# Ten conditioning slots multiplied inside the two layers, and expert slots of 4 MB in a ring of three

## The chip, the cores and the metric

The kernel is one program on one core of a Trainium2 chip. The metric is the device time of one execution in microseconds. Three executions of the kernel before took 2242.32, 2244.37 and 2247.17 us.

## The reference

A token matrix `x` (256 x 1024, fp32) goes through two layers of a first block and then through one layer of a second block.

```
layer l of the first block (l = 0, 1):
    h = rmsnorm(x);  s = h @ w_in            # 1024 -> 3072, cut in 12 slices of 256 columns
    cat = [depthwise conv, stick-breaking attention, retention, short conv](s)
    x = x + rmsnorm(cat @ w_out)             # 1024 -> 1024
    x = x + rmsnorm(ffn(rmsnorm(x)))         # ffn_up, conv over time, gating, ffn_down
second block:
    mod  = silu(c)     @ ada_w + ada_b       # 1024 -> 6144: shift 1, scale 1, gate 1, shift 2, scale 2, gate 2
    modc = silu(c_ctx) @ ada_w + ada_b
    u = modulate(rmsnorm(x), sh1, sc1);  uc = modulate(rmsnorm(ctx), sh1c, sc1c)
    y = token_mixer(u, uc);  x = x + g1 * y
    x = x + g2 * moe(modulate(rmsnorm(x), sh2, sc2))   # 32 experts, 4 of them for each token
    return rmsnorm(x)
```

`mod` and `modc` depend on `c`, `c_ctx` and the weights alone, on nothing that the first block computes. `ada_w` is 24 MB in fp32; the kernel cuts it into twelve slots of 512 columns (2 MB each), called 0 to 11 here.

## The kernel before

**Weights and their ring.** SyncE loads all weights in one fixed order. In the layers and in the mixer of the second block the unit of loading is a half slot of 1 MB; five places form a ring (`RING`), and half `g` waits in `half_used` until half `g - 5` has been used. `LAYER_SLOTS` and `B2_SLOTS` give the order. For the weights of `in`, `up` and `down`, used means split: ScalarE rounds a unit (a quarter of a slot) into a high part (L901, in the second block L995), VectorE subtracts to get the low part (L1231, L1401), and TensorE multiplies in three passes (`PASSES`). Three units are buffered, so `split_until(n)` runs up to three units ahead of TensorE. For `out` used means that the output projection has read it: the first slot at `slot_free`, the second when the bank `("M", 3)` is filled. For an `ada` slot it means that its product is done. Every engine works through its own list in order, so a wait on SyncE or ScalarE holds up all that stands behind it.

**A layer.** `project(0)` to `project(5)` make the twelve slices (items `("s", i)`), with small attention matmuls between. Then come `("I", h)`, `("SB", c)`, the output projection in four parts into banks 4 to 7 (items `("M", i)`, `tokens_down`), with `("CM", 0)` and `("CV", 0)` for the norm of the conv branch between them. After it ScalarE and VectorE both execute

```
split_until(MIX_UNITS + UNIT_BUFFERS - 1)      # units 24, 25, 26: those of ("up", 0)
rms_of_banks(l, "M")                           # ScalarE L868; on VectorE: add_normed, then normalise
```

while TensorE runs filler matmuls (`keep_clock`), waits for the new `x` and for its normalised rows, transposes them (`("F", i)`, L1832), runs filler again, and starts the FFN (66 units with eleven rounds of gating).

**The second block.** TensorE multiplies slots 0 to 3 first, stacked in four column groups of 32 (`ada`). ScalarE copies each result out, `ada_follow` turns it into columns of `modT` with four narrow matmuls (shift and scale), or adds its four partial rows and spreads the sum over all partitions with one wide matmul (gate, slots 4, 5, 10, 11). VectorE adds the bias (L1421) and makes `scale1` and `shift1` (L1434, L1435), which the splits, the modulated rows `u_rows` and so the first projection `mq` wait for. Slots 4 to 11 are multiplied between the projections `mq`, `mk`, `mv` and `mo`.

**The experts.** Sixteen pairs of experts pass through one loop. The whole ring region (12 MB) then holds six places of 2 MB; piece `(w1, x, q)` or `(w2, x, q)` is a quarter or a half of the matrix of expert `x` of the pair. TensorE computes both experts side by side in the two halves of the array and waits for both pieces of a step `q` together (`expert_slot`, L726). SyncE waits on `expert_slot_free` for each place (L807 to L810).

## Time and profile before

| | |
|---|---|
| three executions | 2242.32, 2244.37, 2247.17 us |
| the profiled execution, its own time | 2252.0 us |
| its span, first to last instruction | 2250.2 us |
| TensorE busy | 2079.9 us (92%) |
| VectorE, ScalarE busy | 847.5 us, 651.96 us |
| moved from HBM | 587.27 MB |
| two layers | about 0 to 693 us |
| second block up to the experts | about 699 to 1297 us |
| expert loop | about 1297 to 2239 us |

The page of the profile gives busy times over the whole span; a window gives them for a stretch, with the granted clock of TensorE (1.00 is full speed) and what the DMA moved. A timeline row merges like instructions that follow one another: start, length, engine, line, operation, tile written and tiles read, count, and in brackets the idle time just before with what ended it. The chain of waits lists, in order of time, which work each piece of the span was spent on, followed back from the last instruction. TensorE's helpers record nearly all matmuls at one line (L1812), so the tiles tell them apart: `small` as an input is `siluc`, the operand of the conditioning products.

### The profile page before, as it was taken

Reading aid. Unit: us, or ns where it says so; the run is one execution under the profiler, and the core shown is the slowest. Engines: PE = TensorE matmul, PEld = TensorE weight load, DVE = VectorE, ACT = ScalarE, POOL = GpSimd, SP = SyncE. Lnnn points to the kernel's source line nnn. Section 1 sums busy time; section 2 is a strip of 40 time slices with the busy share of each in tenths; the row PEclk is TensorE's granted clock in tenths of the full one; section 3 lists DMA queues with packets and bytes.
Section 4 is the critical chain, followed back from the end, with each engine's and each line's share of the span. In section 5 each row is a group of like instructions: output and inputs, shape, how many; then the busy total and the mean of one; then the engine's idle time right before and its main releaser. Section 6 shows DMA issues by size and latency. Waiting matters only on the chain.

```text
span 2250.2 us, 28318 instructions
## 1 busy us (share of the span) xinstructions
PE 2079.9 (92%) x11092; PEld 1342.4 (60%) x11092; DVE 847.5 (38%) x1477; ACT 652.0 (29%) x1008; POOL 11.6 (1%) x23
## 2 busy tenths in 40 slices
PE   8899999889998998899999999999999999999997
PEld 7859997849995776776789533333333333333332
DVE  5757676566765334653622211111111111111112
ACT  4435555435555323242431201111111111111111
POOL 0000000000000000000000000000000000000000
PEclk9999999999998999999999999999999999999998
DMA  7325544426546444011233579999999999999995
GB/s 282 113 107 194 187 165 148 142 107 202 183 167 254 173 182 178 29 73 41 93 113 150 243 334 424 417 413 424 422 426 425 429 428 421 430 428 429 421 430 252
DMA packets 55822, 589.63 MB, mean 262 GB/s; under 512 B 6640, under 2 KB 7328, under 8 KB 10000
## 3 DMA queue, kind: packets, MB, share of 16 engines
q1 hardware_dynamic: 53984, 583.09, 63.9%
q0 software_dynamic: 1456, 5.01, 0.8%
q8 instruction: 63, 1.03, 0.2%
q10 hardware_dynamic: 288, 0.24, 0.0%
q14 instruction: 31, 0.25, 0.0%
HBM read 587.27 MB, written 1.05 MB: 261 GB/s over the span
## 4 chain that ended last, share of the span: by engine, by line
PE 73%; DMA 15%; DVE 6%; issue 3%; ACT 2%; SPq 0%; DVEq 0%; ACTq 0%
PE psum L1812 45%; PE psum L2209 20%; DMA slots<-exp_w_dram 14%; PE psum L2199 3%; PE psum L2224 2%; PE psum L2309 2%; DVE split_weights L1401 1%; ACT work L868 0%; DVE work L1527 0%; DMA slots<-ffn_up_dram 0%; DVE split_weights L1231 0%; DVE split_rows L1209 0%; PE psum L2120 0%; SPq L810 0%; PE psum L1832 0%
## 5 line engine op out<-in xcount | busy, mean ns | idle before, releaser
L2209 PE MATMUL psum<-slots,work 128*64 128x512 f32 x3072 | 688.4, 603 | 69.8 <-DMA slots<-exp_w_dram 69.8
L2209 PEld LDWEIGHTS psum<-slots,work 128*64 128x64 f32 x3072 | 227.8, 138 | 506.7 <-issue 506.7
L1812 PE MATMUL psum<-split_rows,split_weights 128*128 128x256 f32 (+1 forms) x3744 | 494.2, 294 | 23.0 <-DVE split_weights L1231 10.2
L1812 PEld LDWEIGHTS psum<-split_rows,split_weights 128*128 128x128 f32 x3744 | 476.9, 194 | 44.5 <-issue 12.8
L1231 DVE TENSOR_TENSOR split_weights<-slots,split_weights 128x1024 fp32r<-128x1024 f32 x180 | 219.0, 1223 | 154.9 <-ACT split_weights L901 154.1
L901 ACT ACTIVATE split_weights<-slots 128x1024 fp32r<-128x1024 f32 x180 | 189.8, 1058 | 224.8 <-PE psum L1812 187.3
L1812 PE MATMUL psum<-split_weights,split_rows 128*128 128x512 f32 x1008 | 234.7, 393 | 2.3 <-DVE split_weights L1401 2.3
L882 ACT ACTIVATE work<-psum 128x512 f32<-128x512 f32 (+2 forms) x180 | 94.6, 537 | 434.6 <-PE psum L2209 291.3
L1812 PEld LDWEIGHTS psum<-split_weights,split_rows 128*128 128x128 f32 x1008 | 190.0, 190 | 44.4 <-DVE split_weights L1401 2.7
L1812 PE MATMUL psum<-work 128*128 128x128 f32 (+9 forms) x992 | 159.3, 341 | 23.0 <-DVE work L1563 6.9
L1771 DVE TENSOR_SCALAR work<-psum 128x512 f32<-128x512 f32 x32 | 22.0, 688 | 406.1 <-PE psum L2209 406.1
L1812 PEld LDWEIGHTS psum<-work 128*128 128x128 f32 (+2 forms) x992 | 130.0, 201 | 55.6 <-issue 40.3
L1146 ACT ACTIVATE work<-work 128x512 f32<-128x512 f32 x32 | 20.2, 631 | 475.4 <-DVE work L1771 475.4
L1766 DVE TENSOR_SCALAR work<-psum,small 128x128 f32<-128x128 f32 x64 | 21.9, 404 | 281.8 <-PE psum L1812 281.8
L1401 DVE TENSOR_TENSOR split_weights<-slots,split_weights 128x1024 fp32r<-128x1024 f32 x64 | 76.4, 1221 | 110.4 <-ACT split_weights L995 110.3
L995 ACT ACTIVATE split_weights<-slots 128x1024 fp32r<-128x1024 f32 x64 | 66.8, 1055 | 111.2 <-DMA slots<-w_in_dram 63.8
L1812 PE MATMUL psum<-slots,work 128*128 128x512 f32 x192 | 87.3, 614 | 3.2 <-ACT work L882 1.6
L1812 PE MATMUL psum<-const 128*128 128x384 f32 (+2 forms) x218 | 76.5, 495 | 11.2 <-DVEq L1804 6.7
L1370 DVE SCALAR_TENSOR_TENSOR work<-psum,work 128x254 f32<-128x254 f32 (+1 forms) x176 | 76.6, 477 | 1.6
L1812 PEld LDWEIGHTS psum<-slots,work 128*128 128x128 f32 x192 | 37.4, 197 | 49.2 <-issue 47.1
L2199 PE MATMUL psum<-work 128*128 128x512 f32 (+1 forms) x136 | 65.8, 627 | 0.5 <-ACT work L882 0.5
L1812 PEld LDWEIGHTS psum<-const 128*128 128x128 f32 (+1 forms) x218 | 41.3, 198 | 41.2 <-issue 15.8
(237 smaller groups left out, 1330.0 us busy)
## 6 DMA issues: line engine op xcount, KB each, us to landing
slots<-exp_w_dram SPq DMA_DIRECT2D x192, 2048.0 KB, 16.3
slots<-w_in_dram SPq DMA_DIRECT2D x56, 1024.0 KB, 5.0
slots<-ffn_up_dram SPq DMA_DIRECT2D x44, 1024.0 KB, 4.8
slots<-ada_w_dram SPq DMA_DIRECT2D x24, 1024.0 KB, 7.0
slots<-ffn_down_dram SPq DMA_DIRECT2D x20, 1024.0 KB, 4.8
slots<-w_out_dram SPq DMA_DIRECT2D x12, 1024.0 KB, 4.9
slots<-w_branch_a_dram SPq DMA_DIRECT2D x4, 1024.0 KB, 8.0
slots<-w_branch_b_dram SPq DMA_DIRECT2D x4, 1024.0 KB, 5.1
```

Of the source, the lines that this page charges most:

```text
L882: nc.scalar.activation(out_, in_, func, **kw).then_inc(evacuated[bank_of(key)], 1)
L901: nc.scalar.activation(unit_weights(n, 0), raw, ACT.Copy).then_inc(w_high_ready, 1)
L995: nc.scalar.activation(unit_weights2(n, 0), unit_weights2(n, None), ACT.Copy).then_inc(w_high_ready, 1)
L1231: nc.vector.tensor_tensor(unit_weights(n, 1), unit_weights(n, None)[0], unit_weights(n, 0), ALU.subtract).then_inc(w_split, 1)
L1370: ins = nc.vector.scalar_tensor_tensor(out=o, in0=b[:, c * T:(c + 1) * T - k], scalar=cols[:, at:at + 1], in1=o, op0=ALU.mult, op1=ALU.add)
L1401: nc.vector.tensor_tensor(unit_weights2(n, 1), unit_weights2(n, None), unit_weights2(n, 0), ALU.subtract).then_inc(w_split, 1)
L1771: nc.vector.tensor_scalar(glu[n], take(dve, ("GLU", n), it), LIMIT, None, ALU.min).then_inc(evacuated[bank_of(("GLU", n))], 1)
L1812: return nc.tensor.matmul(out_, lhsT, rhs, start=first, stop=last)
L2199: return nc.tensor.matmul(psum[:, i, :], lhsT, rhs, start=first, stop=True, skip_group_check=True)
L2209: return nc.tensor.matmul(b[rows, :], lhs[:, rows], rhs, start=first, stop=last, skip_group_check=True)
L2224: nc.tensor.matmul(b, pick_e, b1_rows[:, c0:c0 + 512], start=True, stop=False, skip_group_check=True)
L2309: ins = nc.tensor.matmul(b[:, c * T:(c + 1) * T], hT_split[:, v, 4 * j + k, c * P:(c + 1) * P], wu[a][:, k, :], start=j + c + k + q == 0, ...
```

## The change

`ada_w` is reordered on the host so that ten slots come first; five are multiplied in each of the two layers (`modulation`), from slots `mod` that are put into `LAYER_SLOTS`. The products of mod 0 and mod 1 stand inside `project(4)` and `project(5)`, those of mod 2 and 3 behind the output projection, in place of six filler matmuls, and that of mod 4 with the columns of the second pair behind the FFN's transposes, in place of five. ScalarE copies the results out (`mod_rows_out`), `modulation_columns` turns four of them into columns of `modT`, and the fifth of each layer is one half of gate 1, kept in `g1_kept`. Silu of `c` moves into the layer. Slots 10 and 11 (gate 2) stay where they were in the second block; slots 0 to 9 leave it. In the expert loop the matrices of a pair are interleaved on the host, so that one load of 4 MB brings the pieces of both experts for a step; six loads a pair go through three places in place of twelve through six.

```diff
-LAYER_SLOTS = [("in", s) for s in range(6)] + [("out", s) for s in range(2)]
+N_MOD = 5
+LAYER_SLOTS = [("in", s) for s in range(5)] + [("mod", 0), ("in", 5), ("mod", 1), ("out", 0), ("out", 1)]
+LAYER_SLOTS += [("mod", i) for i in (2, 3, 4)]
+OUT_SLOT = LAYER_SLOTS.index(("out", 0))
+FFN_SLOT = len(LAYER_SLOTS)
...
-LAYER_BANKS += [("s", 6, 6), ("s", 7, 7), ("RQ", 0, 0), ("RK", 0, 1), ("s", 8, 2), ("s", 9, 3)]
+LAYER_BANKS += [("s", 6, 6), ("s", 7, 7), ("RQ", 0, 0), ("RK", 0, 1), ("s", 8, 2), ("mod", 0, 4), ("s", 9, 3)]
 LAYER_BANKS += [("RS", h, 4 + h) for h in range(4)]
-LAYER_BANKS += [("s", 10, 0), ("s", 11, 1)]
+LAYER_BANKS += [("s", 10, 0), ("mod", 1, 2), ("s", 11, 1)]
 LAYER_BANKS += [("I", h, 2 + h) for h in range(4)]
 LAYER_BANKS += [("RO", 0, 0), ("SB", 0, 6), ("SB", 1, 7)] + [("M", i, 4 + i) for i in range(4)]
-LAYER_BANKS += [("CM", 0, 1), ("CV", 0, 2), ("RT", 0, 3)]
-LAYER_BANKS += [("F", i, i) for i in range(4)]
+LAYER_BANKS += [("CM", 0, 1), ("MT", 0, 3), ("CV", 0, 2), ("RT", 0, 3)]
+LAYER_BANKS += [("mod", 2, 0), ("mod", 3, 1)] + [("F", i, i) for i in range(4)] + [("mod", 4, 4), ("MT", 1, 5), ("MT", 2, 6)]
 LAYER_BANKS += [("U", g, (2 * (g // 2)) % 4 + g % 2) for g in range(6)]
...
-B2_BANKS += [("ada", 0, 0), ("ada", 1, 1), ("mT", 0, 2), ("ada", 2, 0), ("ada", 3, 1)]
 B2_BANKS += [("XT", i, i) for i in range(4)] + [("CT", i, 4 + i) for i in range(4)]
-B2_BANKS += [("mq", 0, 0), ("mq", 1, 1), ("ada", 4, 6), ("ada", 5, 7)] + [("mk", h, 2 + h) for h in range(4)]
-B2_BANKS += [("mg", 0, 6), ("mR", 4, 0), ("mR", 5, 1), ("gates", 0, 2), ("ada", 6, 2), ("ada", 7, 3)]
+B2_BANKS += [("mq", 0, 0), ("mq", 1, 1)] + [("mk", h, 2 + h) for h in range(4)]
+B2_BANKS += [("mg", 0, 6), ("gates", 0, 2)]
 B2_BANKS += [("mv", i, 4 + i) for i in range(4)]
-B2_BANKS += [("F", 9, 0), ("GT", 0, 1), ("GT", 1, 2), ("mT", 1, 3), ("ada", 8, 0), ("ada", 9, 1)]
+B2_BANKS += [("F", 9, 0), ("GT", 0, 1), ("GT", 1, 2)]
 B2_BANKS += [("mv", 4 + i, 4 + i) for i in range(4)]
 B2_BANKS += [("ada", 10, 2), ("ada", 11, 0)] + [("mo", i, 4 + i) for i in range(4)]
...
 
-PAIR_SLOTS = [("w1", x, q) for q in range(4) for x in (0, 1)] + [("w2", x, q) for q in range(2) for x in (0, 1)]
+PAIR_SLOTS = [("w1", q) for q in range(4)] + [("w2", q) for q in range(2)]
 PLACE_OF_HALF = {s: i for i, s in enumerate((5, 6, 7, 8, 9, 10, 11, 3, 4, 0, 1, 2))}
-PAIR_RING = 6
+PAIR_RING = 3
 PACKED_KINDS = [slot for slot in B2_SLOTS if slot[0] not in ("ada", "wa", "wb", "wo")]
 
...
-            elif l == L2 or LAYER_SLOTS[n][0] == "out":
+            elif l == L2 or LAYER_SLOTS[n][0] in ("out", "mod"):
...
 
-            at = WEIGHTS_AT + 2 * HALF * (n % PAIR_RING)
-            return slots[:, at:at + 2 * HALF]
+            at = WEIGHTS_AT + 4 * HALF * (n % PAIR_RING)
+            return slots[:, at:at + 4 * HALF]
 
         def expert_slot(pe, it, n, n_k):
 
             pe.wait_ge(expert_loaded[n % PAIR_RING], 16 * (2 * it) + 16 * (n // PAIR_RING + 1))
-            rows = expert_place(n).rearrange("p (k n) -> p k n", k=n_k)
-            return lambda k, c0, c1: rows[:, k, c0:c1]
+            rows = expert_place(n).rearrange("p (x k n) -> p x k n", x=2, k=n_k)
+            return [lambda k, c0, c1, xx=xx: rows[:, xx, k, c0:c1] for xx in (0, 1)]
...
+                elif kind == "mod":
+                    two = [w["ada_w_2"][N_MOD * l + s, h] for h in (0, 1)]
...
             def pair(it, j):
-                for n, (kind, xx, q) in enumerate(PAIR_SLOTS):
-                    src = w["exp_w1_2" if kind == "w1" else "exp_w2_2"][2 * j + xx, q]
-                    sp.wait_ge(expert_slot_free, 12 * it + (n + 1))
+                for n, (kind, q) in enumerate(PAIR_SLOTS):
+                    src = w["exp_w1_2" if kind == "w1" else "exp_w2_2"][j, q]
+                    sp.wait_ge(expert_slot_free, 6 * it + (n + 1))
...
                 evac(("s", 7), l, flat(rv), take(act, ("s", 7), l))
+                act.wait_ge(c_loaded, 16)
+                act.wait_ge(zeros_ready, 3)
+                nc.scalar.activation(siluc[:, :, 0:2], cT, ACT.Silu).then_inc(siluc_ready, 1)
 
                 act.wait_ge(sb_abs, l + 1)
...
+                mod_rows_out(0)
                 evac(("s", 9), l, flat(sc_b), take(act, ("s", 9), l))
...
+                mod_rows_out(1)
                 act.wait_ge(sb_arg, l + 1)
...
                 evac(("RT", 0), l, flat(catT[:, 4:6, :]), take(act, ("RT", 0), l))
                 split_until(MIX_UNITS + UNIT_BUFFERS - 1)
                 rms_of_banks(l, "M")
+                mod_rows_out(2)
+                mod_rows_out(3)
                 rms_of_x(l, 2 * l + 2)
                 act.wait_ge(ffn_par_loaded, 32 * l + 32)
                 high_rows("F", l, 4, COL_FFN_PRE)
+                take(act, ("MT", 1), l)
+                mod_rows_out(4)
 
...
-                act.wait_ge(c_loaded, 16)
-                act.wait_ge(zeros_ready, 3)
-                nc.scalar.activation(siluc[:, :, 0:2], cT, ACT.Silu).then_inc(siluc_ready, 1)
                 def split(n):
                     if n >= UNIT_BUFFERS:
...
-                ada_follow(0)
-                ada(2)
-                ada_follow(1)
-                ada(3)
-                ada_follow(2)
-
-                ada_follow(3)
...
-                        wt = [expert_slot(pe, it, 2 * q + xx, 2) for xx in (0, 1)]
+                        wt = expert_slot(pe, it, q, 2)
...
-                                elif (k, i) == (1, 3):
+                                elif xx and (k, i) == (1, 3):
                                     ins.then_inc(expert_slot_free, 1)
...
                     return ins
 
-                def project(s):
+                def modulation(i):
+
+                    wt = slot_ready(pe, LAYER_SLOTS.index(("mod", i)), l, KC)
+                    if i == 0:
+                        pe.wait_ge(siluc_ready, l + 1)
+                    b = fill(pe, ("mod", i), l)
+                    for k in range(KC):
+                        q = k % 4
+                        ins = mm(b[32 * q:32 * q + 32, :], siluc[:, k, :], wt(k, 0, 512), k < 4, k >= 4)
+                    done(ins, ("mod", i))
+
+                def modulation_columns(i):
+
+                    for j in (2 * i, 2 * i + 1):
+                        after_evacuation(pe, ("mod", j), l)
+                    b = fill(pe, ("MT", i), l)
+                    for c in range(8):
+                        ins = mm(b[:, 2 * c:2 * c + 2], mod_buffers[2 * i + c // 4][:, (c % 4) * P:(c % 4 + 1) * P], mod_pick)
+                    done(ins, ("MT", i))
+
+                def project(s, between=None):
 
                     for i in (2 * s, 2 * s + 1):
+                        if i % 2 and between is not None:
+                            modulation(between)
                         b = fill(pe, ("s", i), l)
                         for j in (0, 1):
                             n = 2 * i + j
...
                 for c in (0, 1):
                     diagonal_scores("RS", l, rkT, rqT, c)
...
                 pe.wait_ge(sb_soft, l + 1)
...
                 mm(b[:, 0:T], ones, conf_sq[:, 0, :], True, False)
                 done(mm(b[:, 0:T], ones, conf_sq[:, 1, :], False, True), ("CV", 0))
                 pe.wait_ge(sc_cat, l + 1)
-                tokens_down("M", l, 7, catT, (6, 7), False, False, None)
+                tokens_down("M", l, OUT_SLOT + 1, catT, (6, 7), False, False, None)
...
-                keep_clock(("F", 0), l, 6)
+                tokens_down("M", l, OUT_SLOT + 1, catT, (4, 5), False, True, None)
+
+                modulation(2)
+                modulation(3)
                 pe.wait_ge(x_tile_ready, 2 * l + 2)
-                keep_clock(("F", 0), l, 3)
-                transposed("F", l, 2, idle=(("D", 0), 5))
+                keep_clock(("F", 2), l, 3)
+                transposed("F", l, 2, idle=lambda: (modulation(4), modulation_columns(1)))
                 for n in range(MIX_UNITS, len(UNITS)):
                     slot, j = UNITS[n]
+                    if n == MIX_UNITS + 1:
+                        after_evacuation(pe, ("mod", 4), l)
+                        b = fill(pe, ("MT", 2), l)
+                        done(mm(b, mod_spread, mod_buffers[4]), ("MT", 2))
                     kind, g = LAYER_SLOTS[slot]
```

## Rows read from the trace of the kernel before

**Rows 1.** The page: TensorE's busy time, and the chain that ended last, by engine.

```profile
PE 2079.9 (92%) x11092; PEld 1342.4 (60%) x11092; DVE 847.5 (38%) x1477; ACT 652.0 (29%) x1008; POOL 11.6 (1%) x23
...
PE 73%; DMA 15%; DVE 6%; issue 3%; ACT 2%; SPq 0%; DVEq 0%; ACTq 0%
```

**Rows 2.** Windows: stretch, length, busy time of each engine, clock, DMA share, GB/s.

```profile
1960.00:2016.00 56.00, 51.42 (x240) 20.70 (x238) 8.58 (x17) 7.51 (x12) 0.00 (x0) 1.00 1.01 429
```

**Rows 3.** The chain of waits in layer 0: start, length, what.

```profile
138.25 4.79 DMA slots<-ffn_up_dram
...
144.09 1.10 ACT work L868 x2
```

**Rows 4.** Timeline of SyncE's DMA issues in the same stretch.

```profile
138.25 8.14 SPq L780 DMA_DIRECT2D slots<-ffn_up_dram  x5
```

**Rows 5.** Timeline of TensorE in the same stretch.

```profile
122.55 1.13 PE L1812 MATMUL psum<-work,const 128*128 128x256 f32 x4 [1.58 <-ACT work L941]
...
131.18 13.90 PE L1812 MATMUL psum<-slots,work 128*128 128x512 f32 x32
...
155.76 3.39 PE L1812 MATMUL psum<-const 128*128 128x384 f32 x10
```

**Rows 6.** Windows with queued loads: 1 MB (two windows), then 2 MB.

```profile
148.00:152.00 4.00, 3.16 (x9) 1.26 (x8) 3.90 (x6) 1.35 (x3) 0.00 (x0) 1.00 1.00 418
...
820.00:832.00 12.00, 12.00 (x55) 9.90 (x54) 5.26 (x10) 2.47 (x3) 0.00 (x0) 1.00 1.01 427
1240.00:1264.00 24.00, 24.00 (x58) 10.61 (x57) 3.30 (x4) 2.52 (x4) 0.00 (x0) 1.00 1.02 434
```

**Rows 7.** Timeline of TensorE in layer 1, slices 9 and following.

```profile
423.51 3.14 PE L1812 MATMUL psum<-split_rows,split_weights 128*128 128x256 f32 x24 [1.87 <-DVE split_weights L1231]
...
435.26 13.28 PE L1812 MATMUL psum<-split_rows,split_weights 128*128 128x256 f32 x96 [2.51 <-DVE split_weights L1231]
```

**Rows 8.** Timeline of ScalarE: the Silu of `c`.

```profile
697.72 1.28 ACT L990 ACT_TABLE_LOAD   x1
699.02 0.23 ACT L990 ACTIVATE small<-small 128x16 f32<-128x16 f32 x1
```

**Rows 9.** Timeline of VectorE at the start of the second block.

```profile
707.60 0.76 DVE L1430 TENSOR_SCALAR work<-work,stats 128x1024 f32<-128x1024 f32 x1
720.80 0.19 DVE L1421 TENSOR_TENSOR small<-psum,work 128x32 f32<-128x32 f32 x1 [12.44 <-PE psum L1812]
...
721.25 0.16 DVE L1435 SCALAR_TENSOR_TENSOR small<-small,work 128x8 f32<-128x8 f32 x1
```

**Rows 10.** Windows in the second block, for the granted clock.

```profile
704.00:708.00 4.00, 0.04 (x1) 0.07 (x1) 2.10 (x5) 3.22 (x8) 0.00 (x0) 0.67 1.00 422
812.00:816.00 4.00, 4.00 (x23) 2.67 (x26) 1.91 (x5) 0.00 (x0) 0.00 (x0) 0.50 0.00 0
```

**Rows 11.** Timeline of TensorE: products, spreads and columns between the projections.

```profile
746.01 3.64 PE L1812 MATMUL psum<-slots,small 128*32 128x512 f32 x32
...
775.17 2.79 PE L1812 MATMUL psum<-work 128*128 128x512 f32 x12
778.37 3.64 PE L1812 MATMUL psum<-slots,small 128*32 128x512 f32 x32 [0.41 <-DVE small L1463]
...
810.80 3.41 PE L1812 MATMUL psum<-work 128*128 128x2 f32 x16
814.14 5.53 PE L1812 MATMUL psum<-slots,small 128*32 128x512 f32 x32
...
841.50 1.84 PE L1812 MATMUL psum<-work 128*128 128x2 f32 x16
```

**Rows 12.** Timeline of TensorE: the fourth piece of the first and last pair.

```profile
1318.75 7.09 PE L2209 MATMUL psum<-slots,work 128*64 128x512 f32 x32 [0.66 <-DMA slots<-exp_w_dram]
...
2206.82 7.09 PE L2209 MATMUL psum<-slots,work 128*64 128x512 f32 x32 [0.60 <-DMA slots<-exp_w_dram]
```

**Rows 13.** One window in the expert loop.

```profile
1425.00:1426.00 1.00, 1.00 (x6) 0.29 (x4) 0.00 (x0) 0.00 (x0) 0.00 (x0) 1.00 0.71 164
```

133 lines of the change are left out of this document (62 added, 71 removed).

## The prediction

> **What bounds the kernel now.** I read the page first. TensorE is busy 92% of the span and most of the chain that ended last is TensorE [rows 1], but a share over the span mixes stages, so I went to the windows and the chain of waits by stage. The two layers (0 to 693 us) and the mixer of the second block (699 to 1237 us) are a chain on TensorE with waits for ScalarE and VectorE in between. The expert stage (from 1297 us) is a chain on the DMA: its engines are at full share while TensorE is idle for a tenth [rows 2]. So a microsecond of TensorE work or of waiting counts in full before 1297 us, whereas after it only the moment at which the stage starts and the rate of its loads count.
>
> **The change, part by part.** The sum is made against the profiled execution (span 2250.2 us, own time 2252.0 us) and then applied as a difference to the median of 2244.4 us.
>
> *1. The loads in the gap of each layer.* This is the largest term, and it comes from SyncE's queue. Between the output projection and the FFN, ScalarE (and VectorE behind it) splits weight units 24, 25 and 26 before it squares the banks of the projection. Unit 26 lies in the second half slot of `("up", 0)`. Today that half is asked for when `slot_free` rises: issued at 138.25 us, landed 4.79 us later, and the squares start at 144.09 us [rows 3]. SyncE issues the others around it [rows 4]. The projection itself ends at 131.18 + 13.90 = 145.1 us [rows 5], so the load hides behind it almost exactly.
>
> In the new order the slots mod 2, mod 3 and mod 4 stand ahead of `("up", 0)`. The ring holds five halves and a half waits for the one five before it. Halves are numbered two per slot: mod 2 is 20 and 21, mod 3 is 22 and 23, mod 4 is 24 and 25, up 0 is 26 and 27. Halves 21 and 22 follow `slot_free`. Halves 23 and 24 follow the end of the projection (145.1 us). Halves 25 and 26 follow the product of mod 2, and half 27 follows the product of mod 3, which itself needs half 23. From 145.1 us five halves (23 to 27) must pass, in order, ahead of unit 26. One alone takes 4.79 us, of which 1.05 MB at the 418 to 427 GB/s of queued 1 MB loads [rows 6] is 2.46 us, so 2.33 us are fixed. The products come soon enough to keep the queue filled (half 23 lands at 149.9, mod 3 is done at 151.7, while half 26 still moves until 157.4). Half 27 lands at 145.1 + 2.33 + 5 x 2.46 = 159.7 us instead of 143.0: **+16.7 us**, and everything behind it on ScalarE (square, root), on VectorE (`add_normed`, `normalise`) and on TensorE (transposes, FFN) waits. If the queue were empty for half 27, the least is 145.1 + 4.8 + 1.8 + 4.8 = 156.5, +13.5 us; if nothing of this showed, 0, the first rival below. Two layers: +33.4 us.
>
> *2. Products inside the projections.* mod 0 comes where TensorE waits 1.87 us for a split [rows 7]. A pair of such products takes 3.64 us [rows 11], so one takes 1.82 and fits. That split is late because of ScalarE's Exp and Ln, and the moved Silu puts a table load and an activation (1.28 + 0.23 us [rows 8]) ahead of them: +1.5. mod 1 stands in the run of 13.28 us without a gap [rows 7]: +1.8. The eight narrow matmuls of MT 0 (1.84 us for eight [rows 11]) stand where TensorE waits 1.58 us for ScalarE [rows 5], and VectorE waits for them too: +0.4. MT 2 is one wide matmul, 13.90/16 = 0.9 us [rows 5], in the FFN's run: +0.9. mod 4 and MT 1 (1.8 + 1.8) replace the filler of 3.4 us behind the transposes [rows 5]: 0 at full clock. Per layer 4.6 us, with bounds of 2 (mod 1 alone on the path) and 7.4 (nothing hidden, no filler gone); two layers +9.2.
>
> *3. Filler taken away.* In the new gap TensorE has nothing from about 152 to 166 us. Rows show what such a gap does: without work from 703 to 708 us the granted clock fell from full (2.4 GHz) to half (1.2 GHz), and it stood at half too during thin work at 812 us [rows 10]. After it, the fillers, the transposes, mod 4 and MT 1 run at half for a while. They have under 1 us of slack before the FFN starts. I take 1.5 us per layer (bounds 0 and 7, the last if all 7 us of that work run twice as long): +3.0. The Trainium skill, "TensorE: Matmul & The Clock Gate", section "Part 1: The HAM clock gate", says an idle array drops to half its clock and needs sustained work to come back; it speaks against taking filler out, and the trace agrees; followed to its end it gives rival C.
>
> *4. The start of the second block.* VectorE has the context rows normalised at 707.60 + 0.76 = 708.4 us and then waits for the four products and their columns. Its scale factors are ready at 721.4 us, 0.4 us after the columns [rows 9]. With `modT` long there they are ready at 708.8 us: **-12.6 us** in front of the same chain (three splits, `u_rows`, first projection). ScalarE's Silu leaves it as well, hidden by the wait for `x`. Bounds -14 and -9 (first projection at half clock).
>
> *5. Products out of the mixer.* The chain there is TensorE without gaps. Taken out are 3.64 (4, 5), 4 x 0.43 = 1.7 of the 2.79 us row (spreads 4 and 5), 3.64 (6, 7), 3.41 (columns 6, 7), 5.53 (8, 9) and 1.84 (columns 8, 9) [rows 11]: 19.8 us. But 3.41 and 5.53 were run at half clock [rows 10] where the same kinds take 1.84 and 3.64; that 3.5 us will be paid by `mv` 1, which moves into the slow stretch. And an evacuation of about 0.6 us ahead of `gates` loses its cover. **-15.7 us**, bounds -19.8 and -13. The load stall ahead of `mo` stays: it hangs on slots 10 and 11, which don't move.
>
> *6. The expert stage.* From the fourth piece of the first pair to that of the last is 2206.82 - 1318.75 = 888.1 us for 15 pairs [rows 12], 59.2 us and 25.17 MB each, 425 GB/s. TensorE always waited for both experts' pieces and gave both back within one matmul, so a 4 MB slot changes neither what it waits for nor the depth of the ring (12 MB). The first halves are now released one matmul later (0.22 us), and once a pair the DMA queue does run low (164 GB/s at 1425 us [rows 13]): +0.2 us for 15 pairs at most, I take +2, bounds -18 (below) and +20 (below). The prefetch (8 MB at 1238 us, 4 MB at 1266 us) is still through before 1297 us, at 434 GB/s [rows 6].
>
> The Trainium skill, "DMA: Bandwidth & Descriptors", section "Anatomy of one DMA", gives some 2 us fixed for each DMA and advises large ones. Were that paid in turn, halving the twelve loads of a pair would save 12 us of it, an estimate. The trace doesn't agree: queued 1 MB and 2 MB loads move 427 and 434 GB/s.
>
> **Sum.** 33.4 + 9.2 + 3.0 - 12.6 - 15.7 + 2 = +19.3 us: 2269.5 us of span, **2263.7 us** for the median. The signs come from one comparison: the second block gives back 28 us once, the gap takes 17 us twice.
>
> **The rivals.**
> - *A. The gap's loads don't hold it up* (faster). If half 27 were there by the projection's end, the sum is 2263.7 - 33.4 = 2230 us. It decides the sign from 7.1 us of delay per layer downward ((33.4 - 19.3)/2). For it: layers use only half of the DMA. Against: it isn't bandwidth over the stage that counts, but which half waits for which, and half 23 can't be issued before the projection ends.
> - *B. Larger loads close the expert stage's gap* (no change). If the stage moved at the 434 GB/s seen at 1240 us, a pair takes 58.0 us: 15 x 1.2 = 18 us less, and my 2 us go: 2244 us. For it: the dip at 1425 us [rows 13]. Against: the dip follows the release of a slot, and its size doesn't change that.
> - *C. The clock stays at half behind each gap* (slower still). 7 us instead of 1.5, twice: 2275 us. For it: at 708 to 719 us thin work didn't bring it back. Against: the filler and the FFN's matmuls are dense.
> - *D. The coarse ring runs dry each pair*, as at 1425 us, by 1.3 us more: 2264 + 20 = 2284 us. Against: the release order is the same.
>
> **Chances.** My forecast 0.62, A 0.12, B 0.10, C 0.10, D 0.06. What this kernel's measurement can tell from no change is 0.2%, 4.5 us. Faster: A and a bit of the rest, 0.14; same: B and a bit, 0.11; slower 0.75. The likeliest case alone is 2255 to 2272 us. The range takes in B and C and leaves out A and D: 2242 to 2278 us.
>
> **What would show it.** In the profile after: (1) in each layer ScalarE's squares of the projection's banks start some 17 us after it ends, the idle before the split of unit 26 put down to a DMA of `ffn_up`; (2) TensorE idle for over 10 us there, at half clock; (3) in the second block the scale factors ready within 1 us of the context rows, and no matmuls with `small` but those of slots 10 and 11; (4) a pair period of 59.2 to 59.4 us. Wrong would make it: unit 26's load landing within 7 us of the projection's end, or a pair period under 58.5 us.

## The result and the profile after

| | before | after |
|---|---|---|
| median | 2242.75 us (12 runs) | 2251.35 us (12 runs) |
| from, to | 2235.99, 2248.06 | 2242.94, 2259.26 |
| ratio | | 1.0044, 95% interval 1.0027 to 1.0062 |
| span of the profiled execution | 2250.2 us | 2255.8 us |
| sum by the prediction | | +19.3 us |

The change makes the kernel slower: 8.6 us between the medians, and 0.44% by the ratio, which compares executions taken side by side. The sign of the forecast and its largest term hold; the whole is less than half of what was forecast. The page of the kernel after, busy time of TensorE and the chain that ended last, answers to [rows 1]:

```profile
PE 2054.0 (91%) x11048; PEld 1325.0 (59%) x11048; DVE 848.4 (38%) x1480; ACT 651.4 (29%) x1009; POOL 11.6 (1%) x23
...
PE 73%; DMA 16%; DVE 6%; issue 3%; ACT 2%; SPq 0%; DVEq 0%; ACTq 0%
```

TensorE has 25.9 us less work and the span is 5.6 us longer, so what was lost was lost in waiting. Where, the chain of waits in layer 0 shows (against [rows 3]):

```profile
133.91 15.59 PE psum L1838 x48
149.50 3.01 issue
152.51 3.30 PE psum L1838 x16
155.83 6.74 DMA slots<-ffn_up_dram
...
163.62 1.10 ACT work L885 x2
```

The squares start at 163.62 us instead of 144.09, directly behind 6.74 us of waiting for the load of unit 26. SyncE's DMA issues (against [rows 4]) show what stands ahead of it:

```profile
99.89 49.99 SPq L796 DMA_DIRECT2D slots<-ada_w_dram  x6
149.93 28.72 SPq L796 DMA_DIRECT2D slots<-ffn_up_dram  x6
...
155.83 0.81 SPq L796 DMA_DIRECT2D slots<-ffn_up_dram  x2
```

The last row is the same view from 153 us on. The first half of `("up", 0)` (half 26) is asked for at 149.93 us, behind the product of mod 2; before, it had been asked for at 95.01 us. The second (half 27), the one with unit 26, is asked for at 155.83 us, behind the product of mod 3, and lands at 162.57; before, these were 138.25 and 143.04 us. TensorE in the same stretch (against [rows 5]):

```profile
112.88 1.58 PE L1838 MATMUL psum<-work 128*64 128x256 f32 x16 [1.33 <-ACT work L961]
115.33 7.10 PE L1838 MATMUL psum<-slots,work 128*128 128x512 f32 x16 [0.87 <-ACT work L899]
...
133.74 13.90 PE L1838 MATMUL psum<-slots,work 128*128 128x512 f32 x32
147.57 1.92 PE L1838 MATMUL psum<-slots,small 128*32 128x512 f32 x16
152.51 3.26 PE L1838 MATMUL psum<-slots,small 128*32 128x512 f32 x16 [3.01 <-issue]
169.19 3.74 PE L1838 MATMUL psum<-const 128*128 128x384 f32 x6 [13.41 <-DVE x_row L1210]
...
179.35 2.87 PE L1838 MATMUL psum<-split_rows,split_weights 128*128 128x256 f32 x22 [0.16 <-issue]
```

The projection ends at 147.64 us and the FFN starts at 179.35: a gap of 31.7 us, with 13.41 us of it without any work. Before it was 145.08 to 159.88 us, 14.8. Two rows of the kernel before, in the same view, matter for the projection:

```profile
107.73 2.63 PE L1812 MATMUL psum<-work 128*64 128x256 f32 x16 [1.33 <-ACT work L936]
111.18 8.92 PE L1812 MATMUL psum<-slots,work 128*128 128x512 f32 x16 [0.83 <-ACT work L882]
```

The same 32 matmuls take 11.55 us before and 8.68 after: their granted clock was 0.57 of full over 108 to 116 us before, and full after. Slices 10 and 11 went the other way. First the row before, then two rows after, with the product of mod 1 between them:

```profile
88.47 11.78 PE L1812 MATMUL psum<-split_rows,split_weights 128*128 128x256 f32 x96 [2.51 <-DVE split_weights L1231]
```

```profile
90.09 7.51 PE L1838 MATMUL psum<-split_rows,split_weights 128*128 128x256 f32 x48 [2.51 <-DVE split_weights L1256]
...
99.39 6.01 PE L1838 MATMUL psum<-split_rows,split_weights 128*128 128x256 f32 x48
```

The 96 matmuls take 13.5 us after against 11.8 before; the granted clock was 0.80 over 88 to 92 us and 0.77 over 92 to 96 us after, and full before. Layer 1 has the same gap as layer 0, and its first FFN unit ran partly at half clock (4.60 us for 24 matmuls that take 3.11 in layer 0):

```profile
502.08 13.90 PE L1838 MATMUL psum<-slots,work 128*128 128x512 f32 x32
...
547.63 4.60 PE L1838 MATMUL psum<-split_rows,split_weights 128*128 128x256 f32 x24 [0.16 <-issue]
```

At the start of the second block, VectorE (against [rows 9]) has its scale factors 0.3 us after the context rows, and TensorE's projections and the end of the mixer (against [rows 11]) follow:

```profile
749.30 0.76 DVE L1456 TENSOR_SCALAR work<-work,stats 128x1024 f32<-128x1024 f32 x1
...
750.19 0.16 DVE L1462 SCALAR_TENSOR_TENSOR small<-small,work 128x8 f32<-128x8 f32 x1
```

```profile
761.86 35.05 PE L1838 MATMUL psum<-split_rows,split_weights 128*128 128x256 f32 x192 [4.07 <-DVE split_rows L1480]
...
831.00 23.68 PE L1838 MATMUL psum<-split_weights,split_rows 128*128 128x512 f32 x96
...
866.02 16.66 PE L1838 MATMUL psum<-split_weights,split_rows 128*128 128x512 f32 x72 [2.10 <-DVE split_weights L1436]
...
887.56 0.41 PE L2033 MATMUL psum<-const 4*128 4x4 f32 x4
```

The stages side by side, each from the start and end of such rows in the two profiled executions, so that each difference is that of one execution against one; the forecasts of the layers are those of steps 1 to 3, +45.6 in all:

| stage | before | after | difference | forecast |
|---|---|---|---|---|
| layer 0 to the projection's end | 145.08 | 147.64 | +2.6 | +3.7 |
| gap, layer 0 | 14.80 | 31.71 | +16.9 | +18.2 |
| FFN 0 to the end of projection 1 | 333.47 | 336.63 | +3.2 | +4.6 |
| gap, layer 1 | 14.85 | 31.65 | +16.8 | +18.2 |
| FFN 1 | 186.74 | 189.07 | +2.3 | +0.9 |
| to the first projection of the second block | 37.98 | 25.16 | -12.8 | -12.6 |
| from there to the end of the mixer's products | 145.05 | 125.70 | -19.4 | -15.7 |
| rest of the second block | 419.30 | 419.36 | +0.1 | 0 |
| expert stage | 952.9 | 948.9 | -4.0 | +2 |
| span | 2250.2 | 2255.8 | +5.6 | +19.3 |

### The profile page after: what moved, and what is told of

It reads as the page before. It is cut to its first block, busy times and chain, and to the rows that moved or that the text cites. A ratio compares the mean times of both kernels' runs of the same rounds, so it can differ in the third digit from the quotient of the medians.

```text
span 2255.8 us, 27802 instructions
## 1 busy us (share of the span) xinstructions
PE 2054.0 (91%) x11048; PEld 1325.0 (59%) x11048; DVE 848.4 (38%) x1480; ACT 651.4 (29%) x1009; POOL 11.6 (1%) x23
## 4 chain that ended last, share of the span: by engine, by line
PE 73%; DMA 16%; DVE 6%; issue 3%; ACT 2%; SPq 0%; DVEq 0%; ACTq 0%
PE psum L1838 44%; PE psum L2203 20%; DMA slots<-exp_w_dram 14%; PE psum L2193 3%; PE psum L2325 3%; PE psum L2218 2%; DVE split_weights L1436 1%; DMA slots<-ffn_up_dram 1%; DMA slots<-w_in_dram 1%; ACT work L885 0%; DVE work L1553 0%; DVE split_weights L1256 0%; PE psum L1858 0%; PE psum L2114 0%; DVE work L1570 0%
## 5 line engine op out<-in xcount | busy, mean ns | idle before, releaser
L2203 PE MATMUL psum<-slots,work 128*64 128x512 f32 x3072 | 680.2, 597 | 74.0 <-DMA slots<-exp_w_dram 74.0
L2203 PEld LDWEIGHTS psum<-slots,work 128*64 128x64 f32 x3072 | 219.2, 137 | 511.4 <-issue 480.3
L1838 PEld LDWEIGHTS psum<-split_rows,split_weights 128*128 128x128 f32 x3744 | 478.8, 195 | 46.7 <-DVE split_weights L1256 13.7
L1838 PE MATMUL psum<-work 128*128 128x128 f32 (+9 forms) x920 | 142.5, 335 | 18.8 <-DVE work L1589 6.9
L1838 PEld LDWEIGHTS psum<-work 128*128 128x128 f32 (+2 forms) x920 | 116.4, 194 | 44.8 <-issue 30.1
L1838 PE MATMUL psum<-const 128*128 128x384 f32 (+2 forms) x174 | 64.9, 518 | 37.5 <-DVE x_row L1210 27.0
L1838 PEld LDWEIGHTS psum<-const 128*128 128x128 f32 (+1 forms) x174 | 34.6, 208 | 64.7 <-DVE x_row L1210 29.4
L2325 PE MATMUL psum<-split_weights,split_rows 128*128 128x256 f32 x480 | 60.4, 288 | 3.6 <-DVE split_weights L1256 3.6
```

What stands on the lines that cost most here:

```text
L1838: return nc.tensor.matmul(out_, lhsT, rhs, start=first, stop=last)
L2203: return nc.tensor.matmul(b[rows, :], lhs[:, rows], rhs, start=first, stop=last, skip_group_check=True)
L2325: ins = nc.tensor.matmul(b[:, c * T:(c + 1) * T], hT_split[:, v, 4 * j + k, c * P:(c + 1) * P], wu[a][:, k, :], start=j + c + k + q == 0, ...
```

## The experiments

All were timed beside the kernel before on the same chip, so the ratio is what compares them across groups.

| run | median, us | ratio to before | 95% interval |
|---|---|---|---|
| a0 changed kernel again | 2249.70 | 1.0040 | 1.0023 to 1.0057 |
| e2 2 MB places | 2256.30 | 1.0076 | 1.0056 to 1.0097 |
| e3 up 0 ahead of mod 4 | 2238.36 | 0.9994 | 0.9975 to 1.0012 |
| e4 splits behind the norm | 2223.19 | 0.9928 | 0.9905 to 0.9951 |
| e1 before with 4 MB places | 2236.93 | 0.9981 | 0.9962 to 0.9999 |
| e9 4 MB places, two loads | 2251.17 | 1.0049 | 1.0032 to 1.0065 |
| e10 2 MB places, filler | 2253.78 | 1.0060 | 1.0037 to 1.0083 |
| e7 filler in the gap | 2249.10 | 1.0044 | 1.0026 to 1.0063 |
| e5 e3 and e4 together | 2232.44 | 0.9963 | 0.9951 to 0.9976 |
| e6 before with e4's edit | 2241.20 | 1.0004 | 0.9994 to 1.0014 |
| e8 before with filler at slice 11 | 2246.47 | 1.0020 | 1.0009 to 1.0032 |
| e12 e4 and mod 3 behind the norm | 2229.99 | 0.9948 | 0.9933 to 0.9964 |
| e13 e12, constants later | 2218.45 | 0.9893 | 0.9868 to 0.9919 |
| e14 e4, constants later | 2221.02 | 0.9903 | 0.9878 to 0.9929 |
| e15 e4 again | 2225.16 | 0.9920 | 0.9896 to 0.9945 |

### The gap: loads, clock or order

**a0** is the changed kernel unedited, the yardstick of its group.

> The changed kernel unaltered, beside the others of this call. By the comparison on record it is 8.6 to 10 us slower than the kernel before. Both theories expect the same here: the second half of the first FFN slot lands about 15 us after the output projection ends, in both layers, and the FFN starts 31 to 32 us after that end instead of 14.8 us.

It repeats the result, 1.0040.

**e3** moves one slot in SyncE's order.

```
-order: mod 2, mod 3, mod 4, up 0, ...
+order: mod 2, mod 3, up 0, mod 4, ...
```

> The changed kernel with the first FFN slot loaded ahead of mod 4 instead of behind it. Theory (halves that pass in order behind the end of the projection): three halves instead of five pass ahead of unit 26, which therefore lands 2.33 + 3 x 2.46 = 9.7 us after the projection ends instead of 14.9 us; 5 us less per layer, 10 us less in all, so about the time of the kernel before (-2 to +1 us). Rival (the delay comes from the product of mod 3 at half clock and from ScalarE's copies, not from the number of halves): no change against the changed kernel, 8 to 10 us over the kernel before.

ScalarE's timeline in e3: units 24 and 25, unit 26, and the squares.

```profile
153.43 2.00 ACT L920 ACTIVATE split_weights<-slots 128x1024 fp32r<-128x1024 f32 x2 [20.34 <-DMA slots<-ffn_up_dram]
155.92 1.06 ACT L920 ACTIVATE split_weights<-slots 128x1024 fp32r<-128x1024 f32 x1 [0.49 <-DMA slots<-ffn_up_dram]
156.88 1.01 ACT L887 ACTIVATE work<-psum 128x1024 f32<-128x1024 f32 x1
```

Two halves fewer ahead of it, and the gap is 26.9 us instead of 31.7: 4.8 us for two halves, 2.4 us each, the 2.46 of the prediction. The time falls by 11.3 us against a0, of which the two gaps explain some 10. So it is the number of queued halves that sets the gap.

**e4** leaves the loads alone and undoes their grip: ScalarE and VectorE normalise first.

```
-split_until(MIX_UNITS + UNIT_BUFFERS - 1)
 rms_of_banks(l, "M")        # VectorE: add_normed, normalise
 ...
 high_rows("F", ...)         # VectorE: low_rows
+split_until(MIX_UNITS + UNIT_BUFFERS - 1)
```

> The changed kernel with the splits of units 24 to 26 behind the rows of the FFN's norm on ScalarE and VectorE instead of ahead of it; loads and products unchanged. Theory: the loads then pass beside the norm (unit 24's half lands 12.1 us after the projection ends, unit 26's 14.6 us, and the norm takes 14.8 us); the FFN starts about 16 us after the projection's end instead of 31.7, 15 to 16 us less per layer and 30 us less in all: 20 to 22 us under the kernel before. Rival: the wait only moves to the first FFN units, and the gain is under 10 us in all.

TensorE's timeline in e4:

```profile
152.39 3.46 PE L1838 MATMUL psum<-slots,small 128*32 128x512 f32 x16 [2.98 <-issue]
155.78 2.20 PE L1838 MATMUL psum<-const 128*128 128x384 f32 x6
...
165.93 4.57 PE L1838 MATMUL psum<-split_rows,split_weights 128*128 128x256 f32 x24 [1.00 <-DVE split_weights L1256]
```

And of ScalarE's, its copy of mod 3:

```profile
155.92 0.60 ACT L899 ACTIVATE work<-psum 128x512 f32<-128x512 f32 x1 [5.85 <-PE psum L1838]
```

The gap is 18.4 us in layer 0 and 18.3 in layer 1, and 26.5 us are back against a0: the changed kernel becomes 0.7% faster than the one before. It isn't 14.8 us, because ScalarE now stands 5.85 us at the bank of the product of mod 3; e12 moves that product.

**e6** asks whether that edit is a gain of its own: the same edit on the kernel before.

> Kernel before with one edit: the splits of units 24 to 26 behind the norm of the projection, nothing of the change. Theory 1 (before, the load of unit 26 was just hidden: it landed 2 us before the projection's end and the squares began as the last bank closed): nothing to gain ahead of the squares, and three splits of 0.6 to 0.9 us now stand between the norm and the FFN's first tap instead: FFN start unchanged within 1 us per layer, 2238 to 2244 us. Theory 2 (the order of ScalarE's queue cost something before as well, so that the gain of 26.5 us in the changed kernel is not all the undoing of the change): FFN start 1.5 us or more earlier per layer, 2236 us or less.

No change, 1.0004. In its profile each gap was 13.3 us instead of 14.8, which the time doesn't show. So e4's gain is, within what the times resolve, the change's loss taken back.

**e7** puts work of TensorE into the hole without touching the loads.

```
 modulation(3)
+keep_clock(("F", 2), l, 17)
```

> The changed kernel with seventeen filler matmuls behind the product of mod 3, where TensorE is idle for 13.4 us in each layer. Theory: the gap is set by the loads, so its length stays at 14.9 us from the projection's end to the landing; what comes back is only the half clock behind it: fillers and transposes at full clock are hidden either way, and the first FFN unit that ran 4.60 us in layer 1 takes 3.1 us; 0 to 3 us less in all (6 to 10 us over the kernel before). Rival (the missing filler is what costs): 8 us or more come back.

TensorE's timeline in e7:

```profile
154.31 11.23 PE L1838 MATMUL psum<-const 128*128 128x384 f32 x34
168.93 3.58 PE L1838 MATMUL psum<-const 128*128 128x384 f32 x6 [3.39 <-DVE x_row L1210]
...
179.10 3.10 PE L1838 MATMUL psum<-split_rows,split_weights 128*128 128x256 f32 x24 [0.16 <-issue]
```

The FFN starts 31.5 us after the projection's end in layer 0 and 32.0 in layer 1, as without filler, although the granted clock was full over 156 to 168 us. Lost clock in the gap is worth no more than the 1.5 us of a first unit, and the time is a0's within the intervals (1.0044 against 1.0040). Rival C is out.

### The products inside the projection

**e8** puts only work of about the length of one product into the kernel before, where mod 1 stands.

```
 # in project(), ahead of each slice i
+if i == 11:
+    keep_clock(("s", 11), l, 3)
```

> Kernel before with six filler matmuls (some 2.2 us at full clock) ahead of projection slice 11 in both layers, where the changed kernel has the product of mod 1; nothing else. It asks why the products inside the projection cost less than forecast. Theory 1 (work there keeps TensorE's clock at full through the short matmuls of SB and the output stage, at half from about 108 to 116 us before): SB 2.63 -> 1.58 us and the first output run 8.92 -> 7.10 us, so +2.2 - 2.9 = -0.7 us per layer: the projection ends 0 to 1 us earlier, the whole within 2 us of before. Theory 2 (the full clock there has another cause, the products of mod 0 or the columns of MT 0): half clock stays at 108 to 116 us, projection end +2 us per layer, the whole +4 us.

TensorE's timeline in e8:

```profile
94.79 2.10 PE L1812 MATMUL psum<-const 128*128 128x384 f32 x6
...
110.11 1.58 PE L1812 MATMUL psum<-work 128*64 128x256 f32 x16 [1.33 <-ACT work L936]
112.47 7.11 PE L1812 MATMUL psum<-slots,work 128*128 128x512 f32 x16 [0.78 <-ACT work L882]
```

The short matmuls run at full clock and take 2.86 us less, for 2.1 us of work added. The projection ends at 144.80 us against 145.08, which by itself says little, as its end in e1 and e6 (147.08 and 143.92 us) shows how far executions lie apart. The rest of the profiles bears the clock out: these 32 matmuls took 8.7 us in both layers of e8 and in all 26 layers of the thirteen profiles with the products, whereas in the six layers of before, e1 and e6, with nothing added, they ran at full clock throughout only once (layer 1 of e1). So in this stretch theory 1 holds: work there pays for itself. The time as a whole went 0.2% up, which the layers don't explain (the FFN of layer 1 started at 507.12 us against 508.20). Seven of its sixteen last steps of a pair (next section) were partly at half clock, against five before; that this is all of it was not tested.

### The expert stage

**e1** is the kernel before with only the 4 MB places; **e2** is the changed kernel with only the 2 MB places back.

> The kernel before with the expert part of the change alone (six loads of 4 MB, three places). After the run with 2 MB places the theory is that 4 MB loads are worth 5 to 8 us in both kernels: the last step of a pair waits 1.87 us instead of 2.05 us, TensorE keeps its clock there (no step of 8.78 us), the pair period goes from 59.2 to 58.9 us, and this kernel is 4 to 8 us faster than the kernel before (ratio 0.9965 to 0.998). Rival (the prediction's view: the size of a place changes nothing): ratio 0.999 to 1.001, period 59.2 us.

> The changed kernel with the expert loop of the kernel before (twelve loads of 2 MB, six places). Theory: the size of the place does nothing to the rate, the 4 us that the changed kernel's expert stage was shorter in its profile are the clock of TensorE in the last pairs, so the time stays within 2 us of the changed kernel (8 to 10 us over the kernel before). Rival: larger loads do save time, some 4 us of it, and this kernel is 12 to 14 us over the kernel before, with a pair period about 0.1 us to 0.25 us longer.

The 4 MB places gain in both: 1.0 to 0.9981 on the kernel before (its interval only just leaves out 1), 1.0076 to 1.0040 on the changed one, 4 and 7 us. The expert stage took 946.8 to 954.1 us in the profiles of before, e2, e6 and e8, 951.0 in the mean, and 937.2 to 950.5, 944.3 in the mean, in the eleven profiles with loads of 4 MB. The last step of a pair shows where. Two rows of TensorE's timeline before, in one pair, then two after:

```profile
1448.45 3.65 PE L2209 MATMUL psum<-slots,work 128*64 128x512 f32 x16 [1.88 <-DMA slots<-exp_w_dram]
...
1458.34 8.78 PE L2209 MATMUL psum<-slots,work 128*64 128x512 f32 x32 [2.06 <-DMA slots<-exp_w_dram]
```

```profile
1337.85 3.65 PE L2203 MATMUL psum<-slots,work 128*64 128x512 f32 x16 [1.92 <-DMA slots<-exp_w_dram]
...
1347.56 7.09 PE L2203 MATMUL psum<-slots,work 128*64 128x512 f32 x32 [1.88 <-DMA slots<-exp_w_dram]
```

With 2 MB places TensorE waits 2.05 us ahead of the last step and in some pairs runs it partly at half clock, 8.78 us instead of 7.09 (a half-clock last step): 18 of the 64 in the profiles of before, e2, e6 and e8. With 4 MB places it waits 1.87 us, and of the 176 in eleven profiles one was such a step, behind a wait of 2.32 us (last pair of e15). From the start of one last step to that of the next, the 17 pairs behind a half-clock last step took 59.0 to 61.4 us, 60.1 in the mean; the 43 other pairs with 2 MB took 58.8 in the mean, and so did the 165 pairs with 4 MB. That is about 5 of the 6.7 us between the stages (17 x 1.3 over four profiles).

The step that opens the second matrix (its first matmuls are the x16 rows above) was partly at half clock too in some pairs, with either size: 9 of 64 and 37 of 176, behind waits of 1.88 to 2.01 us. Two rows of e4:

```profile
1483.09 5.35 PE L2203 MATMUL psum<-slots,work 128*64 128x512 f32 x16 [1.91 <-DMA slots<-exp_w_dram]
...
1492.79 7.09 PE L2203 MATMUL psum<-slots,work 128*64 128x512 f32 x32 [0.18 <-DMA slots<-exp_w_dram]
```

Such a pair loses nothing by it: in all of them the wait for the load ahead of the last step was 0.2 to 0.4 us instead of 1.87 or 2.05. So the clock is lost with both sizes, but with 2 MB places in the last step as well, behind which most of the loss stays (1.3 of 1.7 us).

**e9** fills each 4 MB place by two loads of 2 MB, so that only the grouping differs.

> The changed kernel with its three 4 MB places and its single release for each, but every place filled by two loads of 2 MB. Theory A (it is the number of loads: each one costs some DMA time of its own): the wait of the last step goes back to about 2.05 us, the period to 59.2 us, and the kernel is 12 to 16 us over the kernel before. Theory B (it is the grouping: one wait and one release for both experts): wait 1.87 us, period 58.9 us, 8 to 10 us over the kernel before.

Same time as the changed kernel (1.0049 against 1.0040), periods of 58.70 to 58.84 us but for one of 59.11, the wait 1.95 us and no half-clock last step. So the number of loads isn't what costs the time. It does show in the shortest period: 58.7 us in the profiles of before, e2, e6, e8 and e9, with loads of 2 MB, and 58.3 in all eleven with loads of 4 MB. Last steps of before, then of e7, one pair apart:

```profile
1519.04 7.09 PE L2209 MATMUL psum<-slots,work 128*64 128x512 f32 x32 [2.06 <-DMA slots<-exp_w_dram]
...
1577.77 7.09 PE L2209 MATMUL psum<-slots,work 128*64 128x512 f32 x32 [2.05 <-DMA slots<-exp_w_dram]
```

```profile
1459.73 7.09 PE L2203 MATMUL psum<-slots,work 128*64 128x512 f32 x32 [1.88 <-DMA slots<-exp_w_dram]
...
1518.02 7.09 PE L2203 MATMUL psum<-slots,work 128*64 128x512 f32 x32 [1.87 <-DMA slots<-exp_w_dram]
```

But the 4 MB kernels hold that period in some pairs only (12 of 15 in e7, 2 of 15 in the changed kernel), and their mean of 58.78 us is e9's 58.77. What lengthens the other pairs no run shows.

**e10** is e2 with filler, four matmuls as the trace counts them, ahead of the last step.

> The changed kernel with 2 MB places (as the earlier run, 1.0076) and two filler matmuls of 0.67 us each in the wait ahead of the last step of each pair. Theory A (the loss with 2 MB places comes through TensorE's clock: where the last step runs at half clock, 8.78 instead of 7.09 us, the next release is 1.7 us late and the DMA queue runs low): with filler there is no step of 8.78 us, no period over 60 us, and 3 to 5 us of the 8 us come back (8 to 12 us over the kernel before). Theory B (the rate itself is lower with 2 MB loads): the steps of 8.78 us vanish but the period stays near 59.2 us and the time at 15 to 17 us over the kernel before.

No half-clock last step was left, and the wait behind the filler was 0.57 us. The time went from 1.0076 to 1.0060, but the intervals overlap, and the mean period was 58.96 us, still 0.2 above that of 4 MB places. So the half-clock last steps cost time, but that they are the whole difference is not shown.

### Making the changed kernel better

**e5** is e3 and e4 together.

> Changed kernel with both edits: the slot ('up', 0) ahead of mod 4, and the splits of units 24 to 26 behind the norm of the projection. Theory 1 (with the splits behind the norm, the gap no longer hangs on the load of unit 26 but on ScalarE's and VectorE's own chain, with the product of mod 3 and its copy ahead of the norm): the slot order adds little to the 26.5 us that the later splits alone gave back, 0 to 2 us per layer: 2219 to 2224 us, FFN start 17 to 18.5 us after the projection's end. Theory 2 (the two gains add, since units 25 and 26 must still be split before the FFN's second and third units): another 5 us per layer, about 2213 us. Theory 3 (mod 4 now lands late for TensorE, which has its product ahead of the transposes' banks' release and of the FFN): nothing gained or 1 to 3 us lost per layer, 2225 to 2229 us, with TensorE waiting for a DMA of ada_w before the product of mod 4.

Theory 3, and the loss is larger than it said: in layer 0 TensorE waits 1.53 us for mod 4, in layer 1 6.49 us, and the gap there is 26.0 us. It is 9 us slower than e4. In layer 1 the DMA engines were busy for 0.96 of the time at 190 GB/s over 519 to 523 us, which is what e12 shows next; e5 without the small loads was not run.

**e12** is e4 and moves the product of mod 3 behind the transposes, with ScalarE's copy of it behind the transposed rows.

```
 modulation(2)
-modulation(3)
+keep_clock(("F", 2), l, 6)
 ...
-transposed("F", l, 2, idle=lambda: (modulation(4), modulation_columns(1)))
+transposed("F", l, 2, idle=lambda: (modulation(3), modulation(4), modulation_columns(1)))
```

> Changed kernel with the splits of units 24 to 26 behind the norm, and the product of mod 3 moved too: on TensorE from ahead of the transposes to behind them, ahead of mod 4, with filler (4.0 us) in its old place, and its copy out of the bank on ScalarE behind the copies of the transposed rows. Theory 1 (in the kernel with the later splits, ScalarE waited 5.85 us for the product of mod 3 ahead of the squares of x, and that alone made its gap 18.4 us where the kernel before with later splits has 13.3): the transposes start 6 us after the projection's end, and behind them 5.8 us of products (mod 3, mod 4, columns) end with the rows and the split of unit 24: FFN start 14 to 15 us after the projection's end, -4 us per layer, about 2215 us. Theory 2 (half 27, which now waits for a product of mod 3 that comes later, holds the split of unit 26 and with it the first taps): FFN's first units are held up 2 to 5 us, nothing gained, 2221 to 2226 us.

Each theory was right in one layer. Layer 0 has the gap of theory 1, 14.9 us. In layer 1 the gap is 16.4 us, and then ScalarE waits 9.08 us for the half of unit 26 and TensorE behind it 7.18:

```profile
523.51 1.06 ACT L918 ACTIVATE split_weights<-slots 128x1024 fp32r<-128x1024 f32 x1 [9.08 <-DMA slots<-ffn_up_dram]
```

Windows of e12 in layer 1 (columns as in [rows 2]):

```profile
507.00:511.00 4.00, 4.00 (x42) 1.71 (x40) 2.67 (x7) 3.52 (x9) 2.20 (x4) 1.00 1.01 410
511.00:515.00 4.00, 2.66 (x25) 2.07 (x18) 2.04 (x4) 2.00 (x2) 0.00 (x0) 1.00 0.87 100
```

From 511 to 515 us the DMA engines are busy for 0.87 of the time and move 100 GB/s. GpSimd had asked for nine small loads for the second block (biases, constants, context rows) at 503.6 to 509.2 us.

**e13** is e12, and **e14** is e4, with these nine loads asked for later; **e15** is e4 again beside them.

```
-pool.wait_ge(x_ready, 2 * DEPTH)
+pool.wait_ge(ff_ready, 11 * (DEPTH - 1) + 3)
```

> The kernel of e12 (splits of units 24 to 26 and product of mod 3 behind the norm) with GpSimd's nine loads for the second block asked for three FFN groups later in layer 1 instead of at the residual sum in the gap. Theory 1 (these loads in small packets hold 0.87 of the DMA engines' time at 511 to 515 us for 100 GB/s, and the ring's halves wait behind them): in layer 1 the split of unit 26 waits 2 us instead of 9.08, TensorE's idle of 7.18 us there goes, layer 1 has the gap of layer 0 (14.9 us instead of 16.4): -8 us against e12, 2215 to 2223 us. Theory 2 (layer 1's halves are late for another reason, a slot freed later): unchanged, 2228 to 2232 us, DMA in bytes still low or the issue late.

> The kernel of e4 (only the splits behind the norm) with the same nine loads asked for three FFN groups later in layer 1. In e4 both layers had the same gap (18.4 and 18.3 us) although the small loads ran there too, since its loads are asked for earlier. Theory 1: -0 to -2 us against e4, 2221 to 2224 us. Theory 2 (small loads, now beside the FFN's own loads, hold up a unit there): 1 to 5 us slower than e4.

> The kernel of e4 once more, beside e13 and e14: 2221 to 2226 us, ratio to the kernel before 0.991 to 0.995 if the first measurement holds.

ScalarE's timeline in e13, unit 26 in layer 1, then its windows:

```profile
515.23 1.06 ACT L918 ACTIVATE split_weights<-slots 128x1024 fp32r<-128x1024 f32 x1 [2.06 <-DMA slots<-ffn_up_dram]
```

```profile
511.00:515.00 4.00, 4.00 (x39) 3.16 (x32) 3.29 (x5) 2.17 (x3) 0.00 (x0) 1.00 0.90 320
```

9.08 us of waiting became 2.06, the FFN of layer 1 starts 14.9 us after the projection, and the time falls from 0.9948 to 0.9893 of the kernel before. That is the lowest time measured, 1.1% under the kernel before and 1.5% under the changed kernel, but e14 (0.9903) can't be told from it by the intervals. With e4 alone (e14 against e15) the loads' place makes no difference clear of the intervals.

## Why the prediction was right in sign and wrong in size

Three steps were off, all to the same side. The largest is step 6: it put the expert stage at +2 us, and the stage got 4 to 7 us shorter. Then come step 5's 3.5 us for `mv` 1 and step 2.

*1. The loads in the gap* (+16.7 us each). Right in mechanism and size. Half 27 was forecast 14.6 us behind the projection's end; it landed at 162.57 us, 14.9 behind. e3 measured the price of a half (2.4 us), e4 that this load is what holds the gap, e7 that TensorE's idleness is not. Rival A is out.

*2. The products inside the projections* (+4.6 per layer). Mis-sized: +2.6 us up to the projection's end in layer 0, where 3.7 were forecast, and +3.2 for the FFN and the next projection, where 4.6 were. The step counted what the products add on the path and held all other durations fixed. Its own terms were about right in layer 0: +1.6 for Silu and mod 0 (1.5 forecast), +1.9 for mod 1 (1.8), +0.3 for the rest (0.4). But SB and the first part of the output projection had run at half clock, and with more work ahead of them they ran at full, 2.87 us less; e8 shows this with filler in the product's place. And slices 10 and 11, at full clock before, ran partly at half after, 1.7 us more. So that the sum came within 1.1 us is in part luck, as two changes of clock partly cancel; what brought the second no run tests.

*3. Filler taken away* (+1.5 per layer). It was seen in the first unit of layer 1 (4.60 us against 3.11) and not in layer 0, so 1.5 us of the 3.0; over the profiles with such a gap and no filler in it (after, a0, e2, e9, e10) it came in three of ten layers. The gap itself grew by 16.9, so nothing came on top there. The Trainium skill, "TensorE: Matmul & The Clock Gate", section "Part 1: The HAM clock gate", by which an idle array drops to half its clock, agrees with this trace (granted clock 0.50 over 160 to 172 us). I let it speak against taking filler out; e7 shows how little that was worth where a load sets the end.

*4. The start of the second block* (-12.6). Right: -12.8.

*5. Products out of the mixer* (-15.7). Mis-sized: -19.4. "That 3.5 us will be paid by `mv` 1" was the wrong step. `mv` 1 took 23.68 us against 22.06, so 1.6, and `mo`, which had run partly at half clock, took 16.66 against 18.22. Part of this is one execution: the same stretch took 145.1, 144.8, 141.6 and 141.3 us in the profiles of before, e1, e6 and e8, and 123.7 to 126.4 us in the thirteen profiles with the changed mixer. So the saving lies between 15 and 21 us, 18.8 between the means.

*6. The expert stage* (+2). The sign was wrong: -4 us in the profile, -4 by e1, -7 by e2. The step said "a 4 MB slot changes neither what it waits for nor the depth of the ring". It left out that the wait ahead of the last step gets shorter, 2.05 to 1.87 us, and that this step then stays at full clock; why the wait gets shorter no run shows. That the time doesn't hang on the number of loads was right, within the intervals (e9). The estimate from the Trainium skill, "DMA: Bandwidth & Descriptors", section "Anatomy of one DMA", of 12 us saved for each pair isn't borne out: the page gives its fixed part for loads issued from GpSimd, these are SyncE's, and the most that larger loads showed here was 0.45 us a pair, 58.73 to 58.28, in some pairs. What I missed stood in the timeline of before: last steps of a pair at 8.78 us. I took the mean period of 59.2 us as the DMA's, though 58.73 was the usual one and the pairs behind a half-clock last step raised it. Rival B had the right sign at this place and too high a price; the faster loads that it named show only in the shortest pairs, and the gain in the mean goes with the clock of the last step. Rival D is out: the mean period after was 59.1 us, not 1.3 longer than before.

Together: the layers gave 3.8 us less than forecast (2.6 of it step 2's, 1.5 step 3's, with 0.3 more from the gaps), the mixer 3.7 more back, the experts 6.0 more back, and the start of the second block 0.2; 19.3 - 13.7 is the 5.6 of the profiles. In all three misses there are durations at half clock that I took as fixed.

## What to carry to other kernels

Where a ring of loads is released by work, a slot put ahead of another delays it by its whole place in the chain of releases; count the halves between the release and the load that somebody needs, and look for which instruction needs it: here moving three splits behind the norm gave back 26.5 us, three times what the whole change had lost. Before a sum is made from rows, check for each whether it ran at full clock, since work added or taken away nearby changes that. And small loads on another queue belong where no large load is being waited for.

## What the runs showed of the hardware

- A few small loads take the DMA engines from the large ones: 0.87 share at 100 GB/s (e12), where 410 to 428 were moved in the 8 us ahead of it. A 1 MB half that e13 had 2.06 us late was 9.08 late behind them.
- Ahead of the last step of a pair, waits of 2.03 to 2.32 us stood before all 19 steps partly at half clock, and waits of up to 1.96 us before none. That is no rule for waits: ahead of the step that opens the second matrix, waits of 1.88 to 2.01 us stood before 46 of 240 at half clock. Why 4 MB places shorten the first wait isn't settled.
- A half-clock step costs only where something waits behind it: 1.7 us more in the opening step were taken back in full by the next wait for a load (0.18 instead of 1.87 us), 1.7 us more in the last step made the next pair 1.3 us longer in the mean.
- With 2.1 us of filler some 15 us ahead of them, 32 matmuls took 8.69 us instead of 11.55 (e8): work that cost less than it gave back in its stretch. In one of six layers without it they took 8.68 all the same (layer 1 of e1).
